# Sums of squares of the differential branch as two rounded passes, with their low parts made on VectorE

## The reference, cut to what matters

```
q = rms_norm_2(q.reshape(B, S, H, 2, d), qn_g)        # sum of squares over 64 features
k = rms_norm_2(k.reshape(B, S, H, 2, d), kn_g)        # the same
a = p[:, :, 0] - lam * p[:, :, 1]                     # two softmaxes with a slope on the distance
o = einsum("bhqk,bhkd->bhqd", a, vt)
o = rms_norm_2(o, subln_g) * (1.0 - lambda_init)      # sum of squares over 128 features
o = o.reshape(B, S, DIFF_WIDTH) * jax.nn.silu(gate)
```

## Time and profile before

| | |
|---|---|
| median of 3 runs | 1177.5 us |
| the profiled execution | 1176.51 us |
| its span, first to last instruction | 1174.7 us |
| granted TensorE clock, mean | 0.996 of full speed |
| busy, matmuls (PE) | 1141.0 us |
| busy, weight loads (PEld) | 948.0 us |
| busy, VectorE (DVE) | 815.1 us |
| busy, ScalarE (ACT) | 586.9 us |
| busy, GpSimd (POOL) | 64.2 us |

### The profile page before, as it was taken

One profiled execution on the slowest core, in us unless ns is written; L12 is line 12 of the kernel. 1 busy time (PEld: TensorE's weight loads), 2 busy tenths in 40 slices (PEclk: granted clock), 3 DMA queues, 4 the chain that ended last, 5 costly groups with the idle time before them and its releaser, 6 DMA issues.

```text
span 1174.7 us, 16788 instructions
## 1 busy us (share of the span) xinstructions
PE 1141.0 (97%) x6375; PEld 948.0 (81%) x6380; DVE 815.1 (69%) x1352; ACT 586.9 (50%) x1064; POOL 64.2 (5%) x73
## 2 busy tenths in 40 slices
PE   5899999999999999999999999999999999999998
PEld 5899777766899977777777778888888888788898
DVE  5788555668575237888898885898788686853351
ACT  5663455456564455766657655324554223651320
POOL 1029400101000000000000000000000000000000
PEclk9899999999999999999999999999999999999999
DMA  9967222321454322212222143232222323223221
GB/s 343 345 223 273 91 72 73 90 63 37 148 180 157 108 72 72 72 37 90 72 90 73 36 144 126 72 108 90 90 73 84 132 81 109 97 73 108 104 85 46
DMA packets 36208, 130.41 MB, mean 111 GB/s; under 512 B 4272, under 2 KB 6576, under 8 KB 35616
## 3 DMA queue, kind: packets, MB, share of 16 engines
q1 hardware_dynamic: 32560, 112.74, 29.0%
q0 software_dynamic: 3280, 16.29, 4.2%
q10 hardware_dynamic: 288, 0.31, 0.1%
HBM read 121.72 MB, written 6.29 MB: 109 GB/s over the span
## 4 chain that ended last, share of the span: by engine, by line
PE 87%; DVE 6%; ACT 3%; issue 2%; DMA 2%; SPq 0%; POOL 0%; DVEq 0%; ACTq 0%
PE bank L463 26%; PE bank L465 25%; PE bank L464 25%; PE bank L529 2%; PE bank L677 2%; DMA raw<-in_chunks 2%; DVE wl L1760 1%; PE bank L800 1%; PE bank L705 1%; PE bank L631 1%; ACT qf L1164 1%; DVE ca L2173 1%; DVE stat L1915 0%; PE bank L807 0%; DVE cumt L2441 0%
## 5 line engine op out<-in xcount | busy, mean ns | idle before, releaser
L463 PE MATMUL bank<-hl,wh 128*128 128x512 f32 x888 | 361.7, 407 | 0.9 <-DVE u L2187 0.9
L465 PE MATMUL bank<-hh,wh 128*128 128x512 f32 x888 | 347.1, 391 | 0.0
L464 PE MATMUL bank<-hh,wl 128*128 128x512 f32 x888 | 346.2, 390 | 0.0
L1102 ACT ACTIVATE wh<-raw 128x1024 fp32r<-128x1024 f32 x185 | 191.1, 1057 | 188.9 <-PE bank L465 178.1
L1760 DVE TENSOR_TENSOR wl<-raw,wh 128x1024 fp32r<-128x1024 f32 x185 | 225.2, 1242 | 84.5 <-ACT wh L1102 84.1
L463 PEld LDWEIGHTS bank<-hl,wh 128*128 128x128 f32 x888 | 167.2, 188 | 37.9 <-issue 4.8
L465 PEld LDWEIGHTS bank<-hh,wh 128*128 128x128 f32 x888 | 166.6, 188 | 36.4
L464 PEld LDWEIGHTS bank<-hh,wl 128*128 128x128 f32 x888 | 167.3, 188 | 33.6 <-issue 3.1
L2173 DVE SCALAR_TENSOR_TENSOR ca<-u,vt,ca 128x512 f32<-128x512 f32 x232 | 157.9, 745 | 0.0
L464 PE MATMUL bank<-oh,wl 128*128 128x512 f32 (+1 forms) x256 | 93.9, 367 | 0.0
L465 PE MATMUL bank<-oh,wh 128*128 128x512 f32 (+1 forms) x256 | 93.9, 367 | 0.0
(11 more groups left out here) (323 smaller groups left out, 1676.2 us busy)
## 6 DMA issues: line engine op xcount, KB each, us to landing
raw<-in_chunks SPq DMA_DIRECT2D x193, 512.0 KB, 3.7
ada_a<-in_chunks SPq DMA_DIRECT2D x8, 512.0 KB, 10.9
ada_b<-in_chunks SPq DMA_DIRECT2D x8, 512.0 KB, 8.6
x<-in_x POOLq DMA_DIRECT2D x4, 512.0 KB, 10.5
mem_scratch<-kvm POOLq DMA_DIRECT2D x1, 2048.0 KB, 8.2
x<-in_x POOLq DMA_DIRECT2D x1, 2048.0 KB, 8.1
x_scratch<-x POOLq DMA_DIRECT2D x1, 2048.0 KB, 7.7
kvm<-mem_scratch POOLq DMA_DIRECT2D x1, 2048.0 KB, 9.5
```

Source lines behind the costliest of these rows:

```text
L463: pe.matmul(o, a[0], b[1], start=start, stop=False, **kw)
L464: pe.matmul(o, a[1], b[0], start=False, stop=False, **kw)
L465: return pe.matmul(o, a[0], b[0], start=False, stop=stop, **kw)
L1102: act.activation(wh[:, SLOT[nxt]], raw[:, RAW_SLOT[nxt]], ACT.Copy).then_inc(s.w_hi, 1)
```

## The change

The 14 sums for queries and keys of heads 1 to 7 and the 8 sums for the heads' outputs are each done as two fp32r matmuls instead of one f32 matmul. The square is written a second time by ScalarE, rounded (`sqr`, high part), and VectorE subtracts it from the f32 square to get the low part; TensorE multiplies the ones with the low and with the high part. Head 0's two sums, and all sums outside the stage, stay plain f32. On VectorE the low part of the queries' square comes ahead of tile 0's three weight lows, that of the output's ahead of tile 1's weight low, that of the keys' behind that weight low and ahead of the last 4 taps; that of head 7's output behind the weight lows after the loop. On TensorE the queries' sum moves behind the transpose and two more pieces of tile 1, and the output's sum moves from the end of tile 1 to behind the first three pieces of tile 2. The ones get a tile of their own, loaded by GpSimd's queue behind x, and `cst` shrinks by as much; `blocks` becomes the fp32r tile `blocks_r`, and the new tile `sqr` ([P, 4, S], fp32r) lies beside `kd` in space that x, xT and y use at other times. `SQ` numbers the squares in the order in which they are made.

```diff
-        cst = sb("cst", [P, K_BLOCKS])
-        ident, ones, freq = cst[:, K_IDENT:K_IDENT + P], cst[:, K_ONES:K_ONES + P], cst[:, K_FREQ:K_FREQ + 1]
+        cst, ones_r = sb("cst", [P, K_ONES]), sb("ones_r", [P, P], F32R)
+        ident, freq, ones = cst[:, K_IDENT:K_IDENT + P], cst[:, K_FREQ:K_FREQ + 1], ones_r[:].bitcast(F32)
# TensorE
             def subln(j):
-                pe.wait_ge(s.of_copied, j + 1)
-                total(("sub", j), [rs], ones)
+                pe.wait_ge(s.sq_lo, SQ["sub", j])
+                total(("sub", j), [sqr[:, 1, :], sqr[:, 0, :]], ones_r)
+            def head_sum(what, j):
+                i = "qk".index(what)
+                pe.wait_ge(s.sq_lo, SQ[what, j])
+                total(("dns", 2 * j + i), [sqr[:, 2 * i + 1, :], sqr[:, 2 * i, :]], blocks_r)
                 for tt in range(4):
-                    pieces(fill, at, half)
+                    if tt == 2 and j > 0:
+                        pieces(fill, at, 3)
+                        subln(j - 1)
+                        pieces(fill, at + 3, half - 3)
+                    else:
+                        pieces(fill, at, half)
                     if tt % 2 == 0:
                         diff_scores(j, tt)
-                    if tt in (1, 2) and j < 7:
-                        pe.wait_ge(s.squared, 4 + 2 + 2 * j + tt)
-                        total(("dns", 2 * j + 1 + tt), [norms[:, tt - 1, :]], blocks)
+                    if tt == 2 and j < 7:
+                        head_sum("k", j + 1)
                     if tt in (1, 2):
                         diff_turn(4 * j + tt - 1)
                     pieces(fill, at + half, 2)
                     if tt in (0, 3) and 4 * j + tt > 0:
                         diff_turn(4 * j + tt - 1)
+                    if tt == 1 and j < 7:
+                        head_sum("q", j + 1)
                     if tt == 1 and j > 0:
                         diff_values(j - 1)
                     pieces(fill, at + half + 2, half - 2)
-                    if tt == 1 and j > 0:
-                        subln(j - 1)
# GpSimd's queue
+            pool.dma_start(ones_r[:], t["consts"][:, K_ONES:K_ONES + P].bitcast(F32R)).then_inc(s.ones_in, 16)
# ScalarE
                 act.activation(rs, ps[7][:], ACT.Square).then_inc(s.of_copied, 1)
+                act.activation(sqr[:, 0, :], ps[7][:], ACT.Square).then_inc(s.sq_hi, 1)
                 ...
                         square_q(tt)
+                        act.activation(sqr[:, 2 * tt, :], qf[:, tt, :], ACT.Square).then_inc(s.sq_hi, 1)
# VectorE
+            def square_lo(what, j):
+                i = ("q", "k", "sub").index(what)
+                dve.wait_ge(s.sq_hi, SQ[what, j])
+                ...
+                at = 2 * i % 4
+                dve.tensor_tensor(sqr[:, at + 1, :], norms[:, i, :], sqr[:, at, :].bitcast(F32), ALU.subtract)\
+                   .then_inc(s.sq_lo, 1)
                     if u_ > 0 and (j, tt) != (7, 0):
                         diff_pt_lo(u_ - 1)
+                    if tt == 0 and j < 7:
+                        square_lo("q", j + 1)
                     if tt == 0 and j > 0:
                         banks.wait_full(dve, ("ga", j - 1))
                         ahead(("gb", j - 1))
                         ahead(("ga", j - 1))
-                    if tt < 2 and j < 7:
-                        key = (("dq", "dk")[tt], j + 1)
-                        banks.wait_full(dve, key)
-                        ahead(key)
+                    if tt == 0 and j < 7:
+                        banks.wait_full(dve, ("dq", j + 1))
+                        ahead(("dq", j + 1))
+                    if tt == 1 and j > 0:
+                        square_lo("sub", j - 1)
+                    if tt == 1 and j < 7:
+                        banks.wait_full(dve, ("dk", j + 1))
+                        ahead(("dk", j + 1))
+                        square_lo("k", j + 1)
                     ...
             ahead(("dg", 7))
+            square_lo("sub", 7)
```

More of the change, by code:

```diff
@@ L48 @@
 LAMBDA_INIT = 0.8 - 0.6
-K_IDENT, K_ONES, K_FREQ, K_BLOCKS, K_SEL = 0, 128, 256, 257, 385
+K_IDENT, K_FREQ, K_ONES, K_BLOCKS, K_SEL = 0, 128, 129, 257, 385
 K_COLS = 385 + 4 * P
@@ L100 @@
 SINES = 13
+SQUARES = [name for j in range(8) for name in ([("q", j + 1)] if j < 7 else []) + ([("sub", j - 1)] if j else [])
+           + ([("k", j + 1)] if j < 7 else [])] + [("sub", 7)]
+SQ = {name: n + 1 for n, name in enumerate(SQUARES)}
 Q1 = 9
@@ L144 @@
 SIGNALS = {
-    "const_in": "identity, ones and frequencies loaded", "rows_in": "packed vectors loaded",
+    "ones_in": "ones loaded", "sq_hi": "differential squares: hi", "sq_lo": "lo",
+    "const_in": "identity and frequencies loaded", "rows_in": "packed vectors loaded",
     "tables_in": "masks, distances, slopes and blocks loaded",
@@ L364, in build @@
             [("u", [P, C, PAD + S], F32)])
-        cos, sin, gzb, sel, x, xT, kd, y = shared([("cos", [P, S], F32), ("sin", [P, S], F32), ("gzb", [P, 4, S], F32),
+        cos, sin, gzb, sel, x, xT, kd, sqr, y = shared([("cos", [P, S], F32), ("sin", [P, S], F32), ("gzb", [P, 4, S], F32),
                                                ("sel", [P, 4, P], F32R)],
                                               [("x", [P, T, D], F32)],
-                                              [("xT", [P, C, S], F32)], [("kd", [P, 2, 2, S], F32R)],
+                                              [("xT", [P, C, S], F32)], [("kd", [P, 2, 2, S], F32R), ("sqr", [P, 4, S], F32R)],
                                               [("y", [P, C, S], F32)])
-        cst = sb("cst", [P, K_BLOCKS])
-        ident, ones, freq = cst[:, K_IDENT:K_IDENT + P], cst[:, K_ONES:K_ONES + P], cst[:, K_FREQ:K_FREQ + 1]
+        cst, ones_r = sb("cst", [P, K_ONES]), sb("ones_r", [P, P], F32R)
+        ident, freq, ones = cst[:, K_IDENT:K_IDENT + P], cst[:, K_FREQ:K_FREQ + 1], ones_r[:].bitcast(F32)
         masks = sb("masks", [P, 2, P], BF16)
         ident_b = sb("ident_b", [P, P], BF16)
-        dist, slopes, blocks, xk = shared([("dist", [P, S], F16), ("slopes", [P, 8, P], F16), ("blocks", [P, P], F32)],
+        dist, slopes, blocks_r, xk = shared([("dist", [P, S], F16), ("slopes", [P, 8, P], F16), ("blocks_r", [P, P], F32R)],
                                           [("xk", [P, 2, 2, MEM], F32R)])
@@ L574, in _ @@
                 banks.close(ins, ("mk", h, "k"))
+                if h == 1:
+                    pe.wait_ge(s.ones_in, 16)
                 if h > 0:
@@ L782, in _ @@
                 pe.wait_ge(s.squared, 4 + 1 + pair)
-                total(("dns", pair), [norms[:, pair, :]], blocks, bank=7 - pair)
+                total(("dns", pair), [norms[:, pair, :]], blocks_r[:].bitcast(F32), bank=7 - pair)
                 by_pair("dv", 2, pair, H, 2)
@@ L1012, in _ @@
             pool.dma_start(slopes[:].rearrange("p a n -> p (a n)"), t["consts_h"][:, S:S + 8 * P]).then_inc(s.tables_in, 16)
-            pool.dma_start(blocks[:], t["consts"][:, K_BLOCKS:K_BLOCKS + P]).then_inc(s.tables_in, 16)
+            pool.dma_start(blocks_r[:], t["consts"][:, K_BLOCKS:K_BLOCKS + P].bitcast(F32R)).then_inc(s.tables_in, 16)
             pool.wait_ge(s.h_lo, 8)
@@ L1165, in square_rows @@
                     squares[0] += 1
-            act.dma_start(cst[:], t["consts"][:, 0:K_BLOCKS]).then_inc(s.const_in, 16)
+            act.dma_start(cst[:], t["consts"][:, 0:K_ONES]).then_inc(s.const_in, 16)
             act.dma_start(vt[:], t["vectors"]).then_inc(s.rows_in, 16)
@@ L1242, in _ @@
             act.wait_ge(s.cum_act, 2)
+            act.wait_ge(s.ones_in, 16)
             act.activation(e, e, ACT.Ln, bias=ones[:, 0:1]).then_inc(s.cum_act, 1)
@@ L2200, in diff_mix @@
                 return j
+            def square_lo(what, j):
+                i = ("q", "k", "sub").index(what)
+                dve.wait_ge(s.sq_hi, SQ[what, j])
+                if what == "sub":
+                    dve.wait_ge(s.of_copied, j + 1)
+                else:
+                    dve.wait_ge(s.squared, 4 + 2 * j + i + 1)
+                at = 2 * i % 4
+                dve.tensor_tensor(sqr[:, at + 1, :], norms[:, i, :], sqr[:, at, :].bitcast(F32), ALU.subtract)\
+                   .then_inc(s.sq_lo, 1)
             for j in range(8):
```

## The result

The changed kernel takes 1183.18 us in the median of 4 runs (1182.46 to 1184.82), the kernel before beside it 1177.26 us (1176.69 to 1178.06): a ratio of 1.0054 with a 95% interval of 1.0038 to 1.0070, slower by 5.9 us. The forecast was 1181.2 us. The profiled execution took 1182.46 us with a span of 1180.6 us, 5.9 us more than before, at the same mean granted clock of 0.996.

The account below looks back on a forecast made before the run. TensorE was taken to bound heads 0 to 6 and VectorE head 7, with VectorE's loop only 1.1 us a head behind; terms of -0.5, +4.0, +0.6 and -0.4 made +3.7 us, so 1181.2 us, range 1172 to 1187.

Parts of the forecast that it names:

- VectorE's loop: Loop over VectorE and ScalarE in late heads: 35.6 us plus 1.8 of low parts makes 37.4, against 36.70 before.
- heads 0 and 1: Cheaper sums could gain 1.6 us, but later weight lows use up waits; head 1's maximum comes 0.5 us earlier.
- heads 2 to 6: Five heads each get 1.8 us of low parts, less 5.0 us of existing waits in all: +4.0 us.
- head 7: VectorE is already in the chain; one low part goes in ahead of the taps: +0.6 us.
- behind head 7's maximum (the last sum): Head 7's output sum lies in a stretch bound by TensorE, its low part is early: -0.4 us.
- The start: Smaller `cst` and one more load on GpSimd's queue, ones first used at 31.3 us: nothing, within 0.3 us.
- The low part: One VectorE subtraction of 128x512 takes 0.60 us, or 0.69 without overlap; three in a full head.
- The moved sums: Queries' mean still ahead of the exponentials, output's sum has 1.9 us a head to spare on TensorE: cost nothing.
- a wait at the scores of tile 2 behind the output's sum: Sign that the forecast is wrong: TensorE would be back in the loop and the moved sums not free.
- A: Rival: TensorE stays the bound, the whole 8.8 us comes off, 1168.7 us; chance 0.15.
- B: Rival: heads 1 to 3 keep TensorE's gain, late heads give it back, about 1177.5 us; chance 0.15.
- C: Rival: low parts wait for ScalarE's squares, 1189 us, or 1183.7 if only tile 0's queries; chance 0.08.

Follow-up runs that it names:

- start_only: Kernel before with only the change's loads (ones in their own tile on GpSimd's queue, smaller first table): 1176.18 us, ratio 0.9995 (0.9986 to 1.0003).
- q_early: Changed kernel with the queries' sum back in front of tile 1's transpose and two pieces: 1179.20 us, ratio to before 1.0023.
- dg_first: Changed kernel with tile 0's first weight low ahead of the queries' low part on VectorE: 1179.73 us, ratio to before 1.0027.
- before_taps: Kernel before with tile 1's last four taps moved behind tile 2's transposed probabilities on VectorE: 1177.08 us, ratio to before 1.0011.
- taps0: sub_late plus, on VectorE in tile 0, four taps behind the weight lows and the queries' low part before the last weight low: 1172.75 us.
- one_pass: Kernel before with the 22 sums as one fp32r pass over rounded squares, old places, no low parts: 1170.87 us, ratio 0.9950.
- after_taps: Changed kernel with tile 1's last four taps moved behind tile 2's transposed probabilities on VectorE: 1183.80 us, ratio to before 1.0064.
- before_order: Kernel before with VectorE's order of taps0, TensorE's list untouched: 1179.71 us, ratio to before 1.0026.
- sub_late: Changed kernel, tile 1's last taps moved into tile 2, queries' sum between tile 1's two pieces, output's sum behind tile 2's five pieces: 1174.87 us.

## Why the prediction was right, and where it was not

The direction was right, and so was the reason given for it (three low parts a head lengthen VectorE's loop beyond its 1.1 us of slack). But in the changed kernel that loop is not the one that binds, and the forecast was short by 2.2 us in the profile. Part of the closeness is luck: one term was 3.5 us too small, and the 1.0 us at the start and 0.4 us of VectorE's loop went the other way. Lateness against the kernel before, by the terms of the sum (up to head 7 taken at the maxima of tile 2):

| term | forecast | profile |
|---|---|---|
| up to the stage | 0 | -1.0 (open, see below) |
| heads 0 and 1 | -0.5 | -0.3 |
| heads 2 to 6 | +4.0 | +7.0 |
| head 7 | +0.6 | +0.6 |
| behind head 7's maximum (the last sum) | -0.4 | -0.4 |
| together | +3.7 | +5.9 |

**The start** was put at nothing, within 0.3 us. The change's stage begins 1.0 us earlier. start_only has a median 0.7 us below before's, but its interval includes no gain at all, and one execution against another scatters by as much. Whether this term was off stays open.

**The sum's passes.** 0.46 us was forecast for two; they start at 652.65 and the next piece at 653.12, 0.47.

**The low part.** 0.60 us was taken, with 0.69 as the other end. The starts 642.34 and 642.94 say 0.60. The Trainium skill was cited for the other end (VectorE: DVE Perf Modes, § The DRAIN you can't avoid), and that citation was incomplete: the paragraph ends by saying that a next operation that is not held starts earlier. The rows agree with this ending and not with the rule without it.

**VectorE's loop.** 35.6 + 1.8 = 37.4 to 37.8 us was forecast; q_early shows it alone, 37.3 to 37.7. Its five heads take 187.4 us against before's 183.8, +3.6 where the sum had +4.0.

**The failed step: "The moved sums ... I take nothing."** The prediction priced the queries' mean against the exponentials behind it and found room. The 0.43 us that ScalarE waits for the maximum after the mean (646.80) show that this room exists. What it left out is who else waits for that mean: the product of probabilities and values, in TensorE's own list directly behind the sum, through the bank that the two share. It also left out that the two pieces now ahead of the sum need a weight low that the queries' low part had pushed back. And it took TensorE's spare 1.9 us a head as if it could be spent anywhere; TensorE is tied to VectorE's weight low at 644.21, and from there to the scores it has no slack, so the wait for the bank and the later weight low both delay the scores. The loop so made takes 38.0 us in place of 37.3, over five heads 190.8 - 187.4 = 3.5 us by the unrounded starts. With VectorE's +3.6 that is the +7.0. Undoing either end of the chain (q_early, dg_first) gives most of it back. The prediction did name a sign close to it, "a wait at the scores of tile 2 behind the output's sum"; what shows is VectorE's wait of 0.16 to 0.20 us for those scores.

**The waits that were to go.** The 1.1 us a head of waiting was taken as the slack of VectorE's loop against TensorE, and before_taps confirms TensorE as the bound before. That a small wait is left although TensorE's list is 1.2 us a head shorter is the mark of the new loop, and not of TensorE's amount of work.

**The rivals.** A (TensorE stays the bound, 8.8 us off) fell; even in taps0, where the order suits the low parts, only 4.1 of the 8.8 us arrive. The Trainium skill's rule behind A (Perfetto Trace Analysis, § Identifying the Most-Contended Engine) names TensorE after the change as well, by its matmuls (96%) and by its weight loads (80%), which the page prefers for this engine; shortening its list helped only after the loops had been shortened. B's balance did not come (its two terms give 1177.1 by the prediction's own sum, not 1177.5). C (the queries' rounded square late in tile 0) did not show: VectorE's queries' low part in head 6 starts at 642.34 without a wait. ScalarE's squares do have a price elsewhere, though: 0.44 us a head in one_pass, ahead of the output's sum.

What stays open: one_pass and taps0 stop at 36.1 to 36.8 us a head, above the 34.8 and 35.5 that TensorE's list would give. The traces show small waits there; no run takes them out one by one.

## What to carry to other kernels

When a step is moved, price it by everyone who waits for its result and for its buffer, the next instruction of its own engine first: an accumulation bank that two neighbours in the list share turns the reader's time into a stall. An engine that is busy 97% of the time can have another engine's loop 1 us behind it, and then work that is taken off the first and put on the second is a loss beyond that slack. And a spare microsecond is spare only between the last instruction that waits for the loop and the one that releases it; look for the place before spending it, and test it by taking work out of one engine's loop only, as after_taps did.

## What the runs showed of the hardware

- One idle stretch of TensorE of 2.9 us (up to 680.64 in before_order) was followed by a granted clock of 0.50 for some 6 us and matmuls of 512 columns every 0.43 us in place of 0.23: a wait of 2.9 us cost as much again. In taps0 TensorE was busy for 0.84 of the 2 us from 680 on, and the clock stayed at 1.00. The Trainium skill (TensorE: Matmul & The Clock Gate, § Wait — 56ns, not 53.3ns?) gives 426.7 ns for 512 columns at the lower level, which agrees.
- The length of such a gap alone does not tell what the clock does. Behind the same wait of 2.26 us, in the same stretch of the list, the granted clock stayed at 1.00 in before's execution (gap up to 132.46) and fell to 0.50 in before_taps' (gap up to 132.07). Behind a wait of 2.17 us in head 7 it stayed at 1.00 in before (up to 675.11) and fell to 0.50 in sub_late (up to 671.70). So single executions of nearly one kernel can differ by it.
- A wait on VectorE costs more than its length. Without one the next instruction starts 0.08 us before the one ahead has ended (642.34 + 0.68 against 642.94). The weight low at 652.00 with its wait of 0.28 us would have started at 651.63: 0.37 us.
- Small waits matter here because they recur once a head: the place of the queries' sum was worth 3.6 us (q_early), and one sum of 0.46 us moved by two pieces (sub_late) as much.
